# A mixture-of-experts layer on one core: a second step for four small experts side by side, and gate and up weights read in 8 KB pieces

## What is computed

```python
def routed_experts(h, idx, wts, w_gate, w_up, w_down):
    ...
    def one_group(args):
        xg, e = args
        return (jax.nn.silu(xg @ w_gate[e]) * (xg @ w_up[e])) @ w_down[e]
...
x = x + gate2 * y
```

## Time and profile before

| | |
|---|---|
| median of three executions | 1899.2 us (1898.6 to 1899.38) |
| the profiled execution | 1899.67 us, of which the span from first to last instruction is 1898.0 us |
| mean granted TensorE clock | 0.981 |
| PE busy | 1830.8 us, 96% of the span |
| DVE, ACT, POOL busy | 1137.9, 727.8, 229.4 us |
| moved by DMA | 384.40 MB, mean 203 GB/s |
| PE's share of the chain that ended last | 66% |

### The profile page before, as it was taken

The page is one execution under the profiler, slowest core; times in us unless marked ns, Lnnn a source line. Parts: engine busy times, 40 slices in busy tenths (PEclk is TensorE's granted clock), DMA queues, the critical chain, the costliest instruction groups (busy, mean ns, idle before and its releaser), DMA issues.

```text
span 1898.0 us, 29695 instructions
## 1 busy us (share of the span) xinstructions
PE 1830.8 (96%) x9077; PEld 1381.1 (73%) x9078; DVE 1137.9 (60%) x2171; ACT 727.8 (38%) x1356; POOL 229.4 (12%) x331
## 2 busy tenths in 40 slices
PE   5999999999999999999899999999899999999987
PEld 2787778777567777777588888888477777777632
DVE  3788888888540000001655555556778888888648
ACT  3444444434330000002321221221477777777522
POOL 0100000000000000000101111101322222222111
PEclk7999999999899999999999999999999999999998
DMA  9322212222485444455844344444889869999587
GB/s 373 108 95 112 108 70 106 112 97 91 181 271 192 177 177 177 177 188 185 307 161 151 133 155 144 155 147 166 273 281 354 292 213 337 328 355 313 193 334 316
DMA packets 175851, 384.40 MB, mean 203 GB/s; under 512 B 30184, under 2 KB 104056, under 8 KB 168572
## 3 DMA queue, kind: packets, MB, share of 16 engines
q1 hardware_dynamic: 139836, 321.28, 47.8%
q0 software_dynamic: 19744, 53.89, 7.6%
q10 hardware_dynamic: 16224, 8.65, 1.5%
HBM read 296.80 MB, written 103.73 MB: 211 GB/s over the span
## 4 chain that ended last, share of the span: by engine, by line
PE 66%; DVE 3%; DMA 2%; issue 1%; ACT 1%; ACTq 0%; POOL 0%; DVEq 0%; SPq 0%; POOLq 0%
PE bank L168 18%; PE bank L170 17%; PE bank L169 17%; PE bank L2865 4%; PE bank L2830 2%; PE bank L2008 2%; PE bank L2970 1%; DMA mixer_parts<-oT_split 1%; PE bank L1307 1%; PE bank L2068 1%; DVE late_x L2807 1%; PE bank L2853 1%; DVE expert_down L2802 0%; DMA gathered<-weighted_rows 0%; DMA expert_down<-weighted_rows 0%
## 5 line engine op out<-in xcount | busy, mean ns | idle before, releaser
L168 PE MATMUL bank<-w_mix_hi,hT_hi 128*128 128x512 f32 (+3 forms) x544 | 203.2, 374 | 3.8 <-DVE hT_lo L610 2.5
L1216 DVE SCALAR_TENSOR_TENSOR ma_rows<-tanh_rows,bank 128x512 f32<-128x512 f32 x32 | 20.6, 684 | 310.2 <-PE bank L170 159.9
L2728 DVE TENSOR_TENSOR gate_up_lo<-expert_gate_up,gate_up_hi 128x2048 fp32r<-128x2048 f32 x86 | 196.4, 2288 | 10.9 <-ACT gate_up_hi L2588 9.9
L169 PE MATMUL bank<-w_mix_hi,hT_lo 128*128 128x512 f32 (+3 forms) x544 | 198.8, 365 | 0.0
L170 PE MATMUL bank<-w_mix_lo,hT_hi 128*128 128x512 f32 (+3 forms) x544 | 198.3, 365 | 0.0
L2588 ACT CAST gate_up_hi<-expert_gate_up 128x2048 fp32r (+1 forms) x86 | 165.1, 1923 | 69.0 <-issue 67.2
L168 PE MATMUL bank<-gate_up_hi,gathered_T_hi 128*128 128x512 f32 x352 | 142.5, 405 | 4.9 <-DVE gathered_T_lo L2719 2.1
L170 PE MATMUL bank<-gate_up_lo,gathered_T_hi 128*128 128x512 f32 x352 | 138.4, 393 | 0.0
L169 PE MATMUL bank<-gate_up_hi,gathered_T_lo 128*128 128x512 f32 x352 | 137.9, 392 | 0.0
L168 PEld LDWEIGHTS bank<-w_mix_hi,hT_hi 128*128 128x128 f32 (+1 forms) x544 | 100.6, 185 | 37.0 <-issue 20.3
L170 PEld LDWEIGHTS bank<-w_mix_lo,hT_hi 128*128 128x128 f32 (+1 forms) x544 | 100.6, 185 | 19.1
(11 more groups left out here) (463 smaller groups left out, 3833.9 us busy)
## 6 DMA issues: line engine op xcount, KB each, us to landing
expert_gate_up<-in_w_gate SPq DMA_DIRECT2D x33, 1024.0 KB, 9.6
expert_gate_up<-in_w_up SPq DMA_DIRECT2D x33, 1024.0 KB, 13.1
expert_down<-in_w_down SPq DMA_DIRECT2D x32, 1024.0 KB, 12.7
h_parts<-hT_split SPq DMA_DIRECT2D x16, 1024.0 KB, 5.1
mixer_parts<-oT_split SPq DMA_DIRECT2D x32, 512.0 KB, 8.2
w_ada_part<-in_w_ada SPq DMA_DIRECT2D x16, 1024.0 KB, 10.7
h_parts_b<-hT_split SPq DMA_DIRECT2D x16, 1024.0 KB, 4.9
expert_down<-weighted_rows SPq DMA_DIRECT2D x12, 1024.0 KB, 8.2
```

Source lines behind the costliest of these rows:

```text
L168: nc_mm(out, left[0], right[0], start=first, stop=False)
L169: nc_mm(out, left[1], right[0], start=False, stop=False)
L1216: last = nc.vector.scalar_tensor_tensor(out=ma[:, par, at], in0=tg[:, at], scalar=1.0, in1=ps[2 + n][:, :], op0=ALU.add, op1=ALU.mult)
L2728: nc.vector.tensor_tensor(wg[par][1][:, at], ring[:, bass.ds(slot * GU + n * HG, HG)], wg[par][0][:, at].bitcast(F32), ALU.subtract).then_ ...
```

## The change

- A second quad, after block 3. The list now sets eight experts of 8 to 31 apart by the same rule: the four with the fewest slots in their last block go to the quad at the end, the next four to places 4 to 7, where the new quad takes them. Experts 4 to 7 are in neither. As before, an expert whose last block has 32 slots or fewer has one block fewer.
- Experts 0 to 3 are visited twice: their first blocks at places 0 to 3, what is left of them in four places just ahead of the last quad. So there are 36 places for 32, whether or not a block is left.
- SP's, POOL's, ACT's, DVE's and PE's orders are written out by hand for blocks 2 to 7 around the new quad.
- Gate and up are loaded so that partition p holds rows 8p to 8p + 7, one piece of 8 KB for each matrix. The k-th product then needs columns k, k + 8, k + 16, ... of the gathered rows, so the transposes read every eighth element (`eighth_columns`), for the blocks, the quads and the two blocks ahead. Gate and up lie behind each other in a slot; ACT and DVE put them side by side while they split, and the unsplit products read both (`both_matrices`).
- The list's tables grow: 100 columns for 68, and 36 places.

The diff, cut to its core:

```diff
-WORK = FIXED + 2 * NE
+WORK = FIXED + 3 * NE
+VISITS = NE + FIXED
...
-    ww = ring[:, slot * GU:(slot + 1) * GU].rearrange("p (k c) -> p k c", k=KD)
-    one = lambda t: t[0, bass.ds(e, 1), :, :].rearrange("o (k p) h -> p (o k) h", p=P)
-    sp.dma_start(ww[:, :, 0:EH], one(a["w_gate"])).then_inc(done, 16)
-    sp.dma_start(ww[:, :, EH:], one(a["w_up"])).then_inc(done, 16)
+    ww = ring[:, slot * GU:(slot + 1) * GU].rearrange("p (g k h) -> p g k h", g=2, k=KD)
+    one = lambda t: t[0, bass.ds(e, 1), :, :].rearrange("o (p k) h -> p (o k) h", p=P)
+    sp.dma_start(ww[:, 0, :, :], one(a["w_gate"])).then_inc(done, 16)
+    sp.dma_start(ww[:, 1, :, :], one(a["w_up"])).then_inc(done, 16)
+
+
+def eighth_columns(rows, k):
+
+    return rows.rearrange("m (q k) -> m k q", k=KD)[:, k, :]
+
+
+def both_matrices(slot, k):
+
+    return slot.rearrange("p (g k h) -> p g k h", g=2, k=KD)[:, :, k, :]
...
-        chosen = work[:, THERE, second]
-        step(nc.vector.tensor_scalar(chosen, key, top[:, QUAD - 1:QUAD], None, ALU.is_ge))
-        step(nc.vector.scalar_tensor_tensor(out=order, in0=left, scalar=float(SLOTS_IN_QUAD - 1), in1=chosen, op0=ALU.is_le, op1=ALU.mult))
+        in_b, in_a = work[:, THERE, quad_b], work[:, THERE, quad_a]
+        step(nc.vector.tensor_scalar(in_b, key, top[:, QUAD - 1:QUAD], None, ALU.is_ge))
+        step(nc.vector.tensor_scalar(key, key, top[:, 2 * QUAD - 1:2 * QUAD], None, ALU.is_ge))
+        step(nc.vector.tensor_tensor(in_a, key, in_b, ALU.subtract))
+        step(nc.vector.tensor_scalar(work[:, THERE, between], key[:, FIXED:], -1.0, 1.0, ALU.mult, ALU.add))
+        step(nc.vector.scalar_tensor_tensor(out=order, in0=left, scalar=float(SLOTS_IN_QUAD - 1), in1=key, op0=ALU.is_le, op1=ALU.mult))
         step(nc.vector.tensor_tensor(order, order, early, ALU.add))
         step(nc.vector.scalar_tensor_tensor(out=n, in0=blocks, scalar=1.0, in1=order, op0=ALU.max, op1=ALU.subtract))
-        step(nc.vector.tensor_tensor(work[:, BLOCKS, second], n, chosen, ALU.mult))
-        step(nc.vector.tensor_tensor(work[:, BLOCKS, first], n, work[:, BLOCKS, second], ALU.subtract))
-        step(nc.vector.tensor_scalar(work[:, THERE, first], chosen, -1.0, 1.0, ALU.mult, ALU.add))
+        for part in (quad_a, quad_b):
+            step(nc.vector.tensor_tensor(work[:, BLOCKS, part], n, work[:, THERE, part], ALU.mult))
+        step(nc.vector.tensor_tensor(work[:, BLOCKS, between], n[:, FIXED:], work[:, THERE, between], ALU.mult))
+        step(nc.vector.tensor_copy(work[:, BLOCKS, again], n[:, 0:FIXED]))
...
+        for n in range(RING, 2 * RING):
+            wait_apart(sp, w_lo, (n - RING + 1) * 2, passed)
+            load_gate_up(sp, a, ring, expert_at(n), n % RING, w_in[n % RING])
+            if n >= RING + 2:
+                wait_apart(sp, down, n - RING - 1, passed)
+                load_down(sp, a, downs, expert_at(n - 2), (n - 2) % RING, d_in[(n - 2) % RING])
+        for n in range(RING, 2 * RING):
+            arrived(n % RING, 2)
+        for n in range(2 * RING - 2, 2 * RING):
+            wait_apart(sp, down, n - RING + 1, passed)
+            load_down(sp, a, downs, expert_at(n), n % RING, d_in[n % RING])
+        for n in range(RING, 2 * RING):
+            down_arrived(n % RING, 2)
+        wait_apart(sp, q_tensor, Q_GATE_UP[0], passed)
+        for n in range(2 * RING, 3 * RING):
+            wait_apart(sp, w_lo, last_block(n - RING) * 2, passed)
+            load_gate_up(sp, a, ring, expert_at(n), n % RING, w_in[n % RING])
+            if n == 2 * RING + 2:
+                for slot in range(3):
+                    arrived(slot, 3)
+                wait_apart(sp, q_tensor, Q_OUT[0], passed)
+            if n >= 2 * RING + 2:
+                next_down(n, (n - 2) % RING)
...
+        gather_quad(0, 3)
+        scatter(1, 1)
+        gather(5, 1, 32)
+        scatter(2, 2)
+        wait_apart(pool, q_tensor, Q_TURNED[0], passed)
+        gather(4, 0, 32)
+        scatter(3, 3)
+        gather(6, 2, 32)
+        scatter_quad(0)
...
+                nc.scalar.copy(split_half(wg[par][0], n), loaded_half(slot, n)).then_inc(w_hi, 1)
...
+        quad_silu(0)
+        turned(4, 0)
+        quad_hidden(0)
+        weights(4, 0)
+        quad_weigh(0, 32)
+        quad_records(1)
+        weights(5, 1)
+        for n in (4, 5):
+            records(n, n % 4)
+        silu(4, 0)
+        turned(5, 1)
+        weights(6, 0, (0,))
+        hidden(4, 0)
+        down_high(4)
+        weights(6, 0, (1,))
+        step(5, 1, 32, 48)
...
-                last = nc.tensor.transpose(ps[k // 4][:, (k % 4) * P:(k % 4 + 1) * P], xg[:, par, k * P:(k + 1) * P], ident[:, :])
+                last = nc.tensor.transpose(ps[k // 4][:, (k % 4) * P:(k % 4 + 1) * P], eighth_columns(xg[:, par, :], k), ident[:, :])
...
+        def gate_up_quad(which, ks=range(KD)):
+            if 0 in ks:
+                pe.wait_ge(q_scalar, Q_T[which])
+                pe.wait_ge(q_vector, Q_T_REST[which])
+                pe.wait_ge(w_ready, QUAD_PLACE[which] + QUAD)
+            for k in ks:
                 for c in range(QUAD):
+                    last = nc.tensor.matmul(ps[2][quarter_rows(c), :].rearrange("p (g h) -> p g h", g=2), quad_T[:, k, quarter_rows(c)],
+                                            both_matrices(ring[:, c * GU:(c + 1) * GU], k),
                                             start=(k == 0), stop=(k == KD - 1), tile_position=(0, c * (P // QUAD)))
...
+        gate_up(3, 1)
+        turn_quad(0, 4)
+        out(2, 0)
+        turn_h(3, 1)
+        gate_up_quad(0, range(0, KD // 2))
+        out(3, 1)
+        gate_up_quad(0, range(KD // 2, KD))
+        turn(4, 0, 2)
+        turn_h_quad(0, 4)
+        out_quad(0, 4)
+        gate_up(4, 0)
+        turn(5, 1, 2)
+        turn_h(4, 0)
+        gate_up(5, 1)
+        turn(6, 0, 3)
+        pe.wait_ge(q_scalar, Q_Y[0])
+        out(4, 0)
+        turn_h(5, 1)
+        step(6, 0, 3)
+        step(7, 1, 4)
```

More of the change, by code:

```diff
@@ L2213, in list_blocks @@
     ROW, PLACE, WHO, ENDS, BASE, BLOCKS, THERE, ZERO, TEMP = range(9)
-    fixed, first, second = slice(0, FIXED), slice(FIXED, FIXED + NE), slice(FIXED + NE, WORK)
+    fixed, quad_a, quad_b = slice(0, FIXED), slice(FIXED, FIXED + NE), slice(FIXED + 2 * NE, WORK)
+    between, again = slice(FIXED + NE, 2 * NE), slice(2 * NE, FIXED + 2 * NE)
     count = [0]
@@ L2243, in prepare @@
         step(nc.vector.tensor_copy(work[:, BASE, fixed], work[:, BASE, FIXED:2 * FIXED]))
-        step(nc.vector.tensor_scalar(work[:, BASE, FIXED:2 * FIXED], work[:, BASE, FIXED:2 * FIXED], float(P), None, ALU.add))
-        step(nc.vector.tensor_scalar(work[:, BASE, second], work[:, BASE, second], float(SLOTS_IN_QUAD), None, ALU.add))
+        for at in (WHO, BASE):
+            step(nc.vector.tensor_copy(work[:, at, between], work[:, at, 2 * FIXED:FIXED + NE]))
+            step(nc.vector.tensor_copy(work[:, at, again], work[:, at, fixed]))
@@ L2452, in on_sync @@
         sp.wait_ge(ready["lists"], 1)
+        for n in range(RING, 2 * RING):
[21 more added lines that the diff above has]
+                next_down(n, (n - 2) % RING)
         for slot in range(RING):
-            expert(1, slot, first=True)
-        with sp.Fori(2, NE // RING) as g:
+            expert(3, slot, seen=slot > 0)
+        with sp.Fori(4, VISITS // RING) as g:
             for slot in range(RING):
@@ L2660, in on_scalar, with quad_weigh @@
+        def quad_weigh(which, before):
+            act.wait_ge(q_tensor, Q_OUT[which])
+            act.wait_ge(stored[0], before)
+            act.wait_ge(q_rows_in, (which + 1) * 16 * QUAD)
+            for n in range(2):
+                last = nc.scalar.activation(y[:, 0, n * 512:(n + 1) * 512], ps[5 + n][:, :], ACT.Copy, scale=quad_rows[which][:, 2:3].bitcast(F32))
+            last.then_inc(q_scalar, 1)
         step(1, 1, 16, None)
         records(fore * 2 + 1, LAST[0])
-        step(2, 2, 16, None)
@@ L2663, in on_scalar @@
-        records(fore * 2 + 2, LAST[1])
-        step(3, 3, 16, 16)
-        records(fore * 2 + 3, LAST[2])
-        with act.Fori(1, QUADS) as q:
+        silu(2, 0)
+        turned(3, 3)
+        weigh(1, 1, 16, None)
+        hidden(2, 0)
+        down_high(2)
+        records(3, 3)
+        records(fore * 2 + 2, LAST[1])
+        silu(3, 1)
+        quad_turned(0)
+        weigh(2, 2, 16, 16)
+        hidden(3, 1)
+        down_high(3)
+        records(fore * 2 + 3, LAST[2])
+        weigh(3, 3, 16, 16)
```

266 lines of the change are left out of this document (149 added, 117 removed).

## The result

The changed kernel takes 1924.61 us (median of 4 runs, 1923.38 to 1926.61), the one before 1899.03 (1898.6 to 1899.38) beside it: ratio 1.0134, 95% interval 1.0120 to 1.0149. That is 25.6 us more, where 11.8 were forecast. The profiled execution has a span of 1924.1 us, 26.1 more than before, at a mean granted clock of 0.973.

What follows compares the result with a forecast made beforehand. PE was taken to set the time, with no DMA to spare for one-block experts. Blocks -38.8, quad stretch +43.2, list +1.0, place 30 +1.0, transposes +5 sum to +11.4 us on 1899.2: 1911 us, range 1892 to 1930.

Steps and rivals of the forecast that it cites:

- Four blocks fewer: Expert loop: 40 blocks instead of 44 at 9.71 us each on PE, 38.8 us less.
- The stretch of the quad: Blocks 3 to 6 around the new quad: 37.8 us longer plus 5.4 for low clock, 43.2 us more.
- first wait: Ahead of the new quad's gate and up: PE waits 12 us for four experts' weights, ended by place 7's load.
- second: Ahead of gate_up(4): PE waits 9 us for block 4's late-requested weights, ended by the cast.
- The clock: Behind the two long waits at the new quad: lower granted clock costs 2.7 us each, 5.4 us.
- Rivals 1 and 4: At the quad: no first wait, 1896 or 1891 us (0.17); waits some 9 us shorter, strides cheap, 1899 us (0.10).
- The list, +1.0: Building the list ahead of PE: net three more DVE steps and wider rows, 1.0 us more.
- Term (d): Transposes reading every eighth element: 352 slower weight loads, partly hidden, 5 us more.
- Rival 2: Strided transposes: loads cost in full, +17 us, 1923, or dearer, +54, 1960; chance 0.23, of which 0.05 dearer.
- Term (b): Late one-block experts: place 30's weights asked for two blocks ahead instead of four, 1.0 us more, between 0 and 6.
- credited with 415 GB/s: Weight loads in 8 KB pieces: assumed rate 415 GB/s, taken from pieces of 8 and 4 KB at 400 and 420.
- Rival 3: Late weight stream becomes the bound: 36 loads, 8 KB pieces no faster than 1 KB, about +8 us, 1919; chance 0.12.

Runs made afterwards that it cites:

- quad_half: The changed kernel with places 4 to 7, the new quad's experts, loading only half of gate and up; 1917.2 us, ratio 1.0104.
- strides_only: The old kernel with only the transposes of gathered rows reading every eighth column, pieces still 1 KB; 1898.01 us, ratio 1.0001.
- after: The changed kernel as it stands, with the whole change against the old kernel; 1924.61 us, ratio 1.0134.
- relay_first: The changed kernel with SP passing on the arrivals of places 30 and 31 before its next slot waits; 1929.63 us, ratio 1.0161.
- empties_and_relay: The changed kernel with little loads for empty places 28 and 29 and arrivals of places 30 and 31 passed on earlier; 1923.57 us, ratio 1.0136.
- quad_small_pieces: The changed kernel with the old 1 KB pieces and contiguous transposes, second quad and second visits kept; 1942.2 us, ratio 1.0232.
- after_again: The changed kernel run again unchanged, on the same chip as the run with half of the quad's gate and up; 1926.42 us, ratio 1.0151.
- four_kb_pieces: The changed kernel with gate and up read in 4 KB pieces and transposes reading every fourth column; 1928.43 us, ratio 1.0154.
- before: The old kernel, without the change; 1899.03 us beside the changed kernel, 1897.98 us in the table of piece sizes.
- spin_in_waits: The changed kernel with 16 spare PE products ahead of the quad's gate and up and 12 ahead of gate_up(4); 1927.96 us, ratio 1.0155.

## Why the prediction went as it did

The direction and the order of the events at the quad were right; the size forecast, 11.4 us, was less than half of the 26.3 between the spans.

**Right, within 2 us.** Four blocks fewer, 38.8. The stretch of the quad, 41.3 against 43.2: first wait 11.2 against 12, second 9.0 against 9, each where it was put and ended by what was named. quad_half shows the first to be bytes. The first wait agrees better than it may claim, since the same code had 13.7 us the second time. The clock was priced at 5.4 and is 3.8 by the spare products, and giving it back brought nothing, since the second wait grew by it. Rivals 1 and 4 didn't come.

**The list, +1.0, is 1.3 in its own steps** (1348.42 to 1358.89, 10.5 us, against 9.2) and another 1.4 stood ahead of its first step. The other profiles with the new list start block 0 anywhere from 1364.2 to 1369.5 us, those with the old one from 1365.1 to 1365.5; whether this 1.4 belongs to the change stays open. So does the half clock in block 2, 1.6 us, which the second profile of the same code doesn't have.

**Term (d), +5 for strided transposes, is 0** by strides_only (1.0001). The loads are longer by 51 ns, where 49 had been taken from the nearest rows, but all but 0.01 us a block stays hidden, not two thirds. Rival 2 falls with it, and with it the rule of the Trainium skill, SBUF — State Buffer, "Door 1: The DMA port swizzle", as a price for this kernel: the longer load record is in line with it, the time is unchanged.

**Term (b), +1.0 for place 30, is the first step that failed**: 8.8 us, of which the two profiles of after both have 4.7 to 4.8 as the one wait in block 30 (block 30 longer by 6.7, blocks 31 and 32 by 1.0 and 1.1). It said that the weights are asked for 2 us after block 29 starts (2.5) and land after 7 us, or 11, with 1 us to spare. By its own numbers 2 + 7 = 9 leaves 0.3 us before ACT's 9.26, and 2 + 11 = 13 is 3.7 us too late, so +1.0 was a price for the good case. The cast started 15.4 us after block 29. The term also took landing for use. SP hands an arrival on only behind its own next wait, for the split of the block just ahead, when two places without a block have used up the distance; and the bytes themselves were late as well (12.0 us after the question in relay_first, 9.2 in empties_and_relay, where the two empty visits are small). empties_and_relay takes both away, and block 30 is left with 1.3 us.

**The second failing step is one that the sum didn't have.** The 8 KB pieces were costed where they are loaded, split and transposed, and credited with 415 GB/s; the rows, which share the engines with them, were not looked at again. They land 2.5 us later (7.6 and 10.1), the slack was 2.3 (9.9 less 7.6), and PE lost 8.0 us in blocks 6 to 29 and 1.1 at block 33 by the starts of the blocks, of which the view shows 6.4 as idle. The expectation for quad_small_pieces counts another 1.4 ahead of the quad as a wait for rows; in after that is the half clock of block 2, though after_again does have a wait of 1.4 us for the quad's rows. Rival 3 was near the place but named the wrong thing: it feared 8 KB pieces no faster than small ones. They are faster, and the rows pay for it.

So of the 14.9 us by which the spans' difference exceeds the sum of 11.4, late rows and place 30 make 9.1 and 7.8, the start of block 0 and the clock in block 2 another 1.8 and 1.6, and transposes and quad give back 5 and 1.9; the last 1.5 lie behind block 34.

## What to carry to other kernels

A larger DMA piece buys rate for its own stream and sells latency of everyone else on the same engines: before enlarging one, take the slack of each small transfer beside it (here 2.3 us), and measure its landing again (here 2.1 us later with 4 KB, 2.5 with 8 KB). For a load, ask not only when it lands but who passes the word on and behind which waits that messenger stands. And when two limits stand behind one another, removing either shows nothing; the pair has to be tried before a cause is dropped.

## What the runs showed of the hardware that was not expected

- A weight load of 128 columns at a stride of eight or of four fp32 elements is recorded at 191 and 207 ns instead of 140 (strides_only and after; four_kb_pieces). Eight transposes take 0.80 and 0.87 us instead of 0.79.
- By the records of the single packets, a DMA piece of 8 KB is on its engine for some 310 ns, one of 4 KB for 159, one of 1 KB for 46 (medians). In windows of 5 us between 1400 and 1700 us with the engines' share above 0.98, the median rates were 407 GB/s in after, 403 in four_kb_pieces and 365 in before. With 8 KB instead of 1 KB the first wait was 11.2 and 13.7 us instead of 18.9, 5 to 8 us shorter, where the two rates had been reckoned to give 3.6.
- Spare products of 128x512 took 0.87 us each at the full clock. In spin_in_waits, with at most 0.8 us idle, they kept it there through waits of 9 to 11 us.
